# Two transformer blocks in one kernel: the conditioning product moved from TensorE to GpSimd, in the place of its weight tile

## The reference, cut to what matters

```python
mod = silu(c) @ w_ada + b_ada        # [1024] @ [1024, 6144]: shift, scale, gate (mixer), shift, scale, gate (SwiGLU)
h = rms_norm(x, g_mix) * (1 + scale_1) + shift_1
x = x + gate_1 * token_mixer(h)
h = rms_norm(x, g_ffn) * (1 + scale_2) + shift_2
x = x + gate_2 * swiglu(h)
```

## Time and profile before

| | |
|---|---|
| three runs, median | 1493.82 us (1490.19 to 1495.25) |
| the profiled execution | 1492.98 us, its span 1491.4 us |
| mean granted TensorE clock | 0.957 |
| PE busy | 1295.6 us, 87% |
| VectorE (DVE) busy | 732.7 us, 49% |
| ScalarE (ACT) busy | 260.4 us, 17% |
| GpSimd (POOL) busy | 312.1 us, 21%, nearly all of it the expert loads |

### The profile page before, as it was taken

How to read it: one execution, slowest core, us unless ns; L and a number is a source line. 1 busy time by engine, 2 the same in 40 slices (tenths; PEclk the granted TensorE clock), 3 DMA queues, 4 the chain that set the end, 5 groups by cost and what they waited for, 6 DMA issues and landing times.

```text
span 1491.4 us, 12950 instructions
## 1 busy us (share of the span) xinstructions
PE 1295.6 (87%) x4606; PEld 741.5 (50%) x4606; DVE 732.7 (49%) x1740; ACT 260.4 (17%) x627; POOL 312.1 (21%) x275
## 2 busy tenths in 40 slices
PE   6999999999677778767878697768899988999998
PEld 5757654488433333323333243323347365888843
DVE  2764633147498988895555555564236242011001
ACT  2142211031111111111311111122211332000000
POOL 1100000002244455554334434441000010000000
PEclk9999998999899998999999999999999999999999
DMA  7434446538799999999999989996334633434531
GB/s 260 173 126 170 169 163 246 203 115 318 308 421 421 422 421 415 419 422 421 366 421 422 421 354 414 421 422 249 113 114 166 213 143 113 140 142 141 182 130 54
DMA packets 99422, 400.97 MB, mean 269 GB/s; under 512 B 6368, under 2 KB 9696, under 8 KB 66464
## 3 DMA queue, kind: packets, MB, share of 16 engines
q0 software_dynamic: 37376, 270.29, 43.8%
q1 hardware_dynamic: 61984, 129.87, 24.4%
HBM read 399.09 MB, written 1.05 MB: 268 GB/s over the span
## 4 chain that ended last, share of the span: by engine, by line
PE 59%; DMA 18%; DVE 14%; issue 4%; ACT 2%; POOL 1%; DVEq 0%; POOLq 0%; SPq 0%; PEldq 0%; ACTq 0%
PE ps L482 18%; DMA big<-in_peer_uv,idx_t 16%; PE ps L494 14%; PE ps L732 8%; DVE big L1664 7%; PE ps L930 5%; PE ps L693 4%; PE ps L672 2%; PE ps L575 2%; POOL big L1275 1%; DMA wring<-in_w_in 1%; PE ps L508 1%; PE ps L912 1%; DMA wring<-in_w_up_hg 1%; DVE rows L1585 1%
## 5 line engine op out<-in xcount | busy, mean ns | idle before, releaser
L732 PE MATMUL ps<-big,rows 128*128 128x512 f32 x1024 | 490.8, 636 | 144.7 <-ACT rows L1108 144.7
L732 PEld LDWEIGHTS ps<-big,rows 128*128 128x128 f32 x1024 | 203.3, 203 | 430.6 <-issue 430.6
L1275 POOL DMA_INDIRECT big<-in_peer_uv,idx_t x256 | 295.2, 1153 | 448.0 <-PE ps L732 295.3
L1664 DVE CUSTOM_DVE_ANT_0 big<-big 128x1024 f32<-128x1024 f32 x256 | 308.2, 1226 | 157.7 <-DMA big<-in_peer_uv,idx_t 154.4
L482 PE MATMUL ps<-wring,big 128*128 128x512 f32 (+1 forms) x624 | 274.1, 597 | 13.1 <-issue 5.0
L494 PE MATMUL ps<-big,wring 128*128 128x256 f32 x960 | 210.2, 382 | 1.0 <-DVE big L1329 1.0
L494 PEld LDWEIGHTS ps<-big,wring 128*128 128x128 f32 x960 | 183.9, 192 | 27.2 <-issue 1.9
L482 PEld LDWEIGHTS ps<-wring,big 128*128 128x128 f32 x624 | 119.7, 195 | 155.7 <-issue 144.4
L1102 ACT ACTIVATE small<-small 128x4 f32<-128x4 f32 x64 | 13.1, 205 | 497.1 <-DVE small L1669 497.1
L1108 ACT ACTIVATE rows<-const,small 128x128 f32<-128x128 f32 x256 | 81.8, 390 | 19.2 <-DVE small L1673 17.1
L930 PE MATMUL ps<-wring,big 128*128 128x512 f32 x176 | 75.7, 592 | 0.0
(11 more groups left out here) (236 smaller groups left out, 894.4 us busy)
## 6 DMA issues: line engine op xcount, KB each, us to landing
wring<-in_w_in SPq DMA_DIRECT2D x17, 2048.0 KB, 8.5
wring<-in_w_ada SPq DMA_DIRECT2D x12, 2048.0 KB, 8.6
wring<-in_peer_wq SPq DMA_DIRECT2D x5, 2048.0 KB, 8.2
wring<-in_w_gate SPq DMA_DIRECT2D x5, 2048.0 KB, 7.6
wring<-in_w_up SPq DMA_DIRECT2D x5, 2048.0 KB, 7.7
wring<-in_w_down SPq DMA_DIRECT2D x5, 2048.0 KB, 7.5
wring<-in_w_out SPq DMA_DIRECT2D x4, 2048.0 KB, 7.8
big<-in_peer_uv,idx_t POOLq DMA_INDIRECT x256, 11.7
```

The costliest lines, as they stand in the source:

```text
L732: last = nc.tensor.matmul(banks[h], diag[:, k % DIAGS, :], v_part[:, k % RING, h * 512:(h + 1) * 512], start=False, stop=(k % SLOTS == SLO ...
L1275: pool.indirect_dma_start(pair_ring[:, k % RING, :], None, a["peer_uv"], bass.IndirectOffsetOnAxis(idx_t[:, k:k + 1], 0))\
L1664: nc.vector.tensor_tensor_reduce(u_part[:, k % RING, :], u_part[:, k % RING, :], h_t[:, b, :], 1.0, 0.0, ALU.mult, ALU.add, a_dot[:, i:i + ...
```

## The change

Everything that made, moved and used `ada_part` on PE is gone: 12 times 8 matmuls, 12 moves by ScalarE, the buffer `c_rep` and its copy on VectorE. GpSimd does it instead, with five instructions per tile, linked by semaphore waits: two products of 128 x 2048 in the tile's own place (each chunk with its column of `silu(c)`, repeated along the 512 columns), and three additions that halve the eight chunks to one (128 x 2048, 128 x 1024, 128 x 512). The last writes `ada_rows[i]` or the piece of `mod` and counts `ada_made`. What is left is a sum over partitions, so `group_sum` becomes `ones`, all of it 1; `ada_col` and `ada_row` stay with PE and wait for `ada_made`. SyncE waits for `ada_made` before it loads into a slot that held an ada tile. `ada_rows` is two buffers in turn, so GpSimd waits before part i for `ada_col(i - 2)`.

The eight column parts stand on GpSimd between the memset and the load of `norm_ffn`, the four row parts behind the last expert and ahead of the bias rows.

```diff
-    p += [("a_S", 1, i, g) for i in range(2) for g in range(2)] + [("ada0",)]
+    p += [("a_S", 1, i, g) for i in range(2) for g in range(2)]
...
-    const[0:P:32, C_GROUP:C_END] = 1.0
+    const[:, C_GROUP:C_END] = 1.0
...
                     before = TILES[n - W_SLOTS][0]
-                    if before.startswith("down"):
+                    if before.startswith("ada"):
+                        sp.wait_ge(ada_made, int(before[3:]) + 1)
+                    elif before.startswith("down"):
...
-            def ada_part(i):
-                wt = tile(f"ada{i}", KD, 512)
-                o = begin(f"ada{i}")
-                for c in range(KD):
-                    q = slice(c % 4 * 32, c % 4 * 32 + 32)
-                    last = nc.tensor.matmul(o[q, :], c_rep[:, c, 0:32], wt[:, c, :], start=(c < 4), stop=(c >= 4))
-                last.then_inc(product_done, 1)
...
             def ada_col(i):
 
-                wait_moved(pe, f"ada{i}")
+                pe.wait_ge(ada_made, i + 1)
                 o = begin("ada_col", i)
...
             def ada_row(i):
 
-                wait_moved(pe, f"ada{i}")
+                pe.wait_ge(ada_made, i + 1)
                 o = begin("ada_row", i)
-                nc.tensor.matmul(o, group_sum, mod_part(i), start=True, stop=True).then_inc(product_done, 1)
+                nc.tensor.matmul(o, ones, mod_part(i), start=True, stop=True).then_inc(product_done, 1)
...
             nc.gpsimd.memset(at(big, 14848, 2048), 0.0).then_inc(g_zeroed, 1)
+
+            def ada_part(i):
+                n = TILE_NO[f"ada{i}"]
+                to = ada_rows[i] if i < ADA_COLS else mod_part(i)
+                pool.wait_ge(tile_landed[n % W_SLOTS], 16 * (n // W_SLOTS + 1))
+                slot = n % W_SLOTS * TILE
+                w = wring[:, slot:slot + TILE].rearrange("p (c n) -> p c n", c=KD)
+                for h in range(2):
+                    link(nc.gpsimd.tensor_tensor(w[:, 4 * h:4 * h + 4, :], w[:, 4 * h:4 * h + 4, :],
+                                                 c_s[:, 4 * h:4 * h + 4].unsqueeze(2).to_broadcast([P, 4, 512]),
+                                                 ALU.mult))
+                link(nc.gpsimd.tensor_tensor(w[:, 0:4, :], w[:, 0:4, :], w[:, 4:8, :], ALU.add))
+                link(nc.gpsimd.tensor_tensor(w[:, 0:2, :], w[:, 0:2, :], w[:, 2:4, :], ALU.add))
+                last = nc.gpsimd.tensor_tensor(to, w[:, 0, :], w[:, 1, :], ALU.add)
+                last.then_inc(ada_made, 1)
+
+            pool.wait_ge(c_ready, 1)
+            for i in range(ADA_COLS):
+                if i >= 2:
+                    wait_product(pool, "ada_col", i - 2)
+                ada_part(i)
             wait_moved(pool, "g_O", 0)
...
             wait_product(pool, "experts", NB - 1, 1)
+            for i in range(ADA_COLS, 12):
+                ada_part(i)
             for j in range(2):
```

More of the change, by code:

```diff
@@ L141, in product_list @@
     p += [("a_S", 0, i, g) for i in range(2) for g in range(2)] + [("in_hg", 0)]
-    p += [("a_S", 1, i, g) for i in range(2) for g in range(2)] + [("ada0",)]
+    p += [("a_S", 1, i, g) for i in range(2) for g in range(2)]
     p += [("a_PT", 0, sb, q) for sb in range(NB) for q in range(2)] + [("in_hg", 1), ("a_Y", 0)]
     p += [("a_PT", 1, sb, q) for sb in range(NB) for q in range(2)]
-    p += [("ada1",), ("ada_col", 0), ("a_Y", 1), ("g_diag", 0), ("g_diag", 1)] + level(0)
+    p += [("ada_col", 0), ("a_Y", 1), ("g_diag", 0), ("g_diag", 1)] + level(0)
     p += [("a_YT", 0), ("a_YT", 1), ("ada_col", 1)]
@@ L149, in product_list @@
         p += [(f"in_g{i}", b)] + level(n)
-        if n % 2 and n > 1:
-            p += [(f"ada{i + 1}",)]
         if n % 2 == 0:
             p += [("ada_col", i + 1)] if i else []
-    p += [("in_g3", 1), ("ada5",), ("ada_col", 4), ("g_O", 0), ("g_O", 1)]
-    p += [("ada6",), ("ada_col", 5), ("ada7",), ("ada_col", 6), ("g_OT", 0), ("g_OT", 1), ("ada_col", 7)]
+    p += [("in_g3", 1), ("ada_col", 4), ("g_O", 0), ("g_O", 1)]
+    p += [("ada_col", 5), ("ada_col", 6), ("g_OT", 0), ("g_OT", 1), ("ada_col", 7)]
     p += [(n, b, h) for b in range(NB) for h in range(2) for n in ("up_att", "up_hg")]
@@ L167, in product_list @@
     p += [("d_qT", b) for b in range(NB)] + [("d_kT", b) for b in range(NB)] + [("in2_if",)] + rows("in2_vm")
-    p += [("ada8",), ("ada9",)]
     p += [("d_S", b, i, g) for b in range(NB) for i in range(2) for g in range(2)] + rows("in2_og")
-    p += [("ada10",), ("ada11",), ("ada_row", 8), ("ada_row", 9)]
+    p += [("ada_row", 8), ("ada_row", 9)]
     p += [("m_cols",), ("m_M", 0), ("m_M", 1)] + [("m_S", h) for h in range(GH)]
@@ L328, in two_blocks @@
         one = at(const, C_ONE, 1)
-        group_sum = at(const, C_GROUP, P)
+        ones = at(const, C_GROUP, P)
         eps = at(lane, L_EPS, 1)
@@ L368, in two_blocks @@
         ple_exp, mod_ready, x_ready = sem("ple_exp"), sem("mod_ready"), sem("x_ready")
-        modc_ready = sem("modc_ready")
+        modc_ready, ada_made = sem("modc_ready"), sem("ada_made")
         d_norm, d_max, d_probs, cat_ready = sem("d_norm"), sem("d_max"), sem("d_probs"), sem("cat_ready")
@@ L501, in wait_turned @@
                         wait_moved(pe, name, b, h)
-            def ada_part(i):
-                wt = tile(f"ada{i}", KD, 512)
-                o = begin(f"ada{i}")
-                for c in range(KD):
-                    q = slice(c % 4 * 32, c % 4 * 32 + 32)
-                    last = nc.tensor.matmul(o[q, :], c_rep[:, c, 0:32], wt[:, c, :], start=(c < 4), stop=(c >= 4))
-                last.then_inc(product_done, 1)
             def ada_col(i):
-                wait_moved(pe, f"ada{i}")
+                pe.wait_ge(ada_made, i + 1)
                 o = begin("ada_col", i)
                 for n in range(4):
-                    last = nc.tensor.matmul(o[:, n:n + 1], ada_rows[i][:, n * P:(n + 1) * P], group_sum[:, 0:1],
+                    last = nc.tensor.matmul(o[:, n:n + 1], ada_rows[i][:, n * P:(n + 1) * P], ones[:, 0:1],
                                             start=True, stop=True)
@@ L635, in _ @@
                 level(n)
-                if n % 2 and n > 1:
-                    ada_part(i + 1)
                 if n % 2 == 0 and i:
@@ L976, in move_turned @@
                              src=ps[:, o, :].rearrange("p (c t) -> p c t", c=4))
-            def ada_moves(i):
-                move(ada_rows[i] if i < ADA_COLS else mod_part(i), f"ada{i}")
             def ada_col_out(i):
@@ L1046, in _ @@
             probs(1)
-            ada_moves(0)
             probs_out(0)
@@ L1050, in _ @@
             probs_out(1)
-            ada_moves(1)
             ada_col_out(0)
@@ L1061, in _ @@
                     level_exp(n + 1)
-                if n % 2 and n > 1:
-                    ada_moves(i + 1)
                 if n % 2 == 0 and i:
```

22 lines of the change are left out of this document (1 added, 21 removed).

## The result

Four runs of the changed kernel gave 1558.28 us (1554.19 to 1559.12), four of the kernel before beside it 1492.01 (1489.23 to 1495.25): ratio 1.0437, 95% interval [1.0409, 1.0465]. It is slower by 66.3 us; the forecast was 1579, 21 us more, and the time lies inside the range. The profiled execution took 1558.98 us (span 1557.1, 65.7 more than before).

What follows compares the result with a forecast made beforehand. PE was taken to bound the kernel (87% busy, 59% of the chain). 1493.0 + 59.0 (first block) + 23.7 (second block) + 3.5 (restarts) = 1579 us, the 18.4 us removed already within the shifts; range 1527 to 1607 us.

Steps and rivals of the forecast that it cites:

- What bounds, and the sign: PE bounds, busy 87% of the span; at most 18.4 us removed, yet slower overall, chance 0.96.
- Exclusion with alternation: DVE instructions with two SBUF inputs and POOL's parts exclude each other and alternate, each DVE one waiting for one of POOL's.
- T = 17.7: Time of one ada part on POOL, 17.7 us with hand-overs; allowed from 7 (memset's rate) to 22.
- ada0, +6.8 at the first gate projection (139.4): First block: ada0 meets the four products of `decayed(0)`, so PE reaches the first gate projection 6.8 us late.
- while DVE reads PSUM: no loss: First block: ada1 runs on POOL to 129.1 while DVE reads PSUM, costing nothing.
- ada2 and ada3, decayed(1) at 160.1 and decayed(4) at 199.2: First block: ada2 meets level 1, ada3 level 4; PE late by 20.6, then 28.2 us.
- ada4 hits level 5 (+40.5): First block: ada4 starts at 203.7 behind `ada_col(2)` and meets level 5; PE late by 40.5 us.
- ada7 made at 300.6, up projections at 302.9: End of first block: ada5 to ada7 queue on POOL, 53.1 us plus 5.5 of DVE; up projections +59.0 us.
- Second block, +23.7 at ada_row(11): Four parts on POOL take 70.8 us plus some 2.6 of DVE; `ada_row(11)` and all behind shift 23.7 us.
- DVE's lateness and the bias rows: Second block: DVE's rows up to 17 us late and gates ready 18.6 us later, both hidden behind the later PE work.
- Restarts, 3.5: PE is slower after long waits: 1.75 us for each of two, 3.5 us in all.
- rival B: Exclusion, but DVE's products go through in one run, a level losing one POOL instruction (4.5 us): 1540 to 1560 us, chance 0.12.

Runs made afterwards that it cites:

- the restored 0.69 with memsets: Changed kernel with POOL's products and additions replaced by memsets of about the same total duration: 1524.14 us, ratio 1.0238 to the kernel before.
- whole parts against pieces: Changed kernel with only parts 2 to 5 on POOL, others back on PE: whole instructions 1505.88 us (ratio 1.0120), pieces of 512 columns 1488.94 us (0.9996).
- the late kernel: Only parts 8 to 11 on POOL, PE using 10 and 11 behind out2_1, DVE waiting for them later: 1490.76 us against 1489.15, ratio 1.0013.
- rows alone: Changed kernel with only parts 8 to 11 on POOL, parts 0 to 7 back on PE and ScalarE: 1504.90 us against 1487.73, ratio 1.0128.

## Why the prediction was right, and by how much it was off

- *What bounds, and the sign.* Right. PE had no room for a late partner, and the late partners were DVE and POOL. Removing PE's 18.4 us bought nothing that shows: PE came to its waits earlier and stood longer.
- *Exclusion with alternation* (the forecast's mechanism, chance 0.62). Shown: the timeline of DVE, the restored 0.69 with memsets, and whole parts against pieces. The Trainium skill (SBUF — State Buffer, Who interferes with whom) states that a DVE instruction with two SBUF inputs excludes a GpSimd instruction that reads but not one that only writes; the trace agrees (4.08 and 4.99 us, and 0.69 beside memsets).
- *T = 17.7.* Mis-sized: 15.6 undisturbed. The error was to take the repeated column at the price of a second tensor. The product took 3.6 us where the addition of the same size took 4.5. The memset's rate, from which I had the lower end, was further off on the other side (1.81 us).
- *ada0, +6.8 at the first gate projection (139.4).* It came at 147.49, 8.1 later than forecast. `decayed(0)` itself ended at 106.65, 3.5 earlier than forecast. The step missed DVE's four scalings of the maxima, which took 0.5, 2.9, 3.1 and 4.0 us beside ada1 instead of 0.17, where I wrote "while DVE reads PSUM: no loss": the reductions read PSUM, the scalings between them do not. The transposes started at 120.91, not 114.8, and then ran at 1.2 GHz.
- *ada2 and ada3, decayed(1) at 160.1 and decayed(4) at 199.2.* Measured 162.86 and 201.65. Right to 3 us, but for `decayed(1)` by two errors that nearly cancel: level 1's preparation began 7 us later than forecast (144.85 against 138), and ada2 landed later still (146.49), so that both subtractions were all but through and four instructions met POOL, not six (18.0 us from first to last, 22.1 forecast).
- *ada4 hits level 5 (+40.5).* This step failed. `ada_col(2)` stood behind level 4, whose products took 6.48 us instead of 3.73, so ada4 started at 209.05, 0.3 us after level 5's four products had gone through undisturbed (206.25 to 208.75). It hit level 6, where PE waited 1.9 us; the forecast had 12.3 for level 5 (40.5 less 28.2). In PE's order the second projection of g2 stands before level 6, so ada5 was issued at 226.41 and not at 233.4.
- *ada7 made at 300.6, up projections at 302.9.* 284.33 and 289.71: 7.7 us by the earlier landing of ada5, 8.6 by shorter parts (50.0 us for three, 58.6 forecast), less 3.1, because the last products of the output norm (L1532 to L1534, up to 4.87 us each) were behind even ada7. I had expected PE to stand at `ada_col(6)` and (7), near 40 us together; it stood 11.9 at the first, none at the second, and 15.2 for DVE.
- *Second block, +23.7 at ada_row(11).* 14.3 (and a wait of 14.3, where the prediction looked for near 27). Four parts took 63.3 us (1193.80 to 1257.11) where I had 73.4 with what gets in between; T again. DVE's lateness and the bias rows were hidden, as forecast; the late kernel showed the first once its cover was gone.
- *Restarts, 3.5.* Too few. I counted two, and every wait of PE beyond 5 us was followed by one: 1.7 us in the transposes, 1.7 and 2.75 in levels 1 and 4 (these lie within the first block's 45.8), and 6.0 between `ada_row(11)` and out2 (24.8 us instead of 18.8). The price per restart was not a constant either: behind the same wait, rows alone lost 2.0.

So 86.2 us were forecast and 66.0 came: 13.2 less in the first block (45.8 for 59.0), 9.4 less in the second (14.3 for 23.7), 2.5 more in the restart behind it (6.0 for 3.5). The two steps that missed most are the meeting of ada4 with level 5 and the price of a part. That 1558 lies in the span I gave rival B (1540 to 1560) is a coincidence of sizes: DVE's products did not go through in one run at any level that met a part, except where the part came too late.

## What to carry to other kernels

In these runs POOL was a place for free work only in instructions as short as the wait that DVE can bear, and only where the result is used much later than it is made: here pieces of 512 columns gave back 19 of 66 us, and one later use gave back 15 of 17. Price the partner's instructions one by one, the small ones between reductions too, since a two-column scaling waited here nearly as long as a wide product. And taking work off the bounding engine gains only up to the next arrival; look for the weight load or the norm that stands behind it first (7.4 us off TensorE moved the up projections by 1). Before a small gain is put down to a place in the trace, count from a common event: here profiles differed by up to 7 us in a stretch that no experiment touched.

## What the runs showed of the hardware

- A scaling of 128x2 from SBUF to SBUF took 2.93 to 3.95 us beside POOL's products and additions and 3.51 beside a memset, 0.17 undisturbed. I had not expected it of an instruction with one tensor input. The Trainium skill (VectorE: DVE Perf Modes, Mode 2×_2P) lets such an instruction take both read ports for its one input, and by the Trainium skill (SBUF — State Buffer, Who interferes with whom) an instruction in that mode contends with GpSimd, and the one that issues later is blocked for the whole of the other. The runs agree, down to two columns.
- POOL's product with a repeated column takes 3.6 us for 2048 columns, its addition of two tensors 4.49.
- The waiting party is charged unevenly. Where DVE's products wait for POOL's products or its widest addition, they take 4.08 to 4.99 us instead of 0.69; that addition takes 4.83 instead of 4.49.
- After a wait of 5.6 us (before 201.70) the granted clock was 0.56 for the next 6 us, after 10.9 and 14.3 us it was 0.50 for the next 4 and 5 us; behind the wait of 1.9 us the level took 3.84 instead of 3.73. How long PE then stays slow differs: behind waits of 14.3 and 14.4 us the clock was 0.67 from 5 to 25 us after the start in the changed kernel, and 1.00 from 4 to 20 us after it with rows alone.
